# A hybrid delta-rule and S5 step: a new order of loads and of small work ahead of the first projection

## The reference, cut to what matters

```python
def ada_mod(c, w_mod, b_mod):
    m = (jax.nn.silu(c) @ w_mod + b_mod)[:, None, :]
    shift, scale, gate = jnp.split(m, 3, axis=-1)
...
    hn = rmsnorm(x, norm_mix[i]) * (1.0 + scale) + shift
    out, cv, sd = gdn_mixer(hn, ...)      # proj = hn @ w_in, then a short causal convolution
...
    dt = jnp.exp(log_dt)[:, None]         # S5 tables: no input x in them
    mag = jnp.exp(lr * dt); ang = li * dt
    ab_re, ab_im = mag * jnp.cos(ang), mag * jnp.sin(ang)
```

## Time and profile before

| | |
|---|---|
| median of 3 runs | 1769.54 us (1766.22 to 1769.86) |
| the profiled execution's own time | 1765.61 us |
| its span, first to last instruction | 1763.9 us |
| PE busy | 1484.9 us, 84% of the span |
| DVE busy | 709.5 us, 40% |
| ACT busy | 404.5 us, 23% |
| POOL busy | 116.6 us, 7% |
| mean granted clock of PE | 0.888 of full |
| PE's share of the chain that ended last | 49% |

### The profile page before, as it was taken

One profiled execution on the slowest core, in us unless ns is written; L12 is line 12 of the kernel. 1 busy time (PEld: TensorE's weight loads), 2 busy tenths in 40 slices (PEclk: granted clock), 3 DMA queues, 4 the chain that ended last, 5 costly groups with the idle time before them and its releaser, 6 DMA issues.

```text
span 1763.9 us, 26539 instructions
## 1 busy us (share of the span) xinstructions
PE 1484.9 (84%) x11278; PEld 1160.8 (66%) x11278; DVE 709.5 (40%) x1207; ACT 404.5 (23%) x559; POOL 116.6 (7%) x162
## 2 busy tenths in 40 slices
PE   3799999968876888965999958998999955999955
PEld 2577777746675826743878846776777734778744
DVE  1657895055553054144111147779701140111106
ACT  2344551013222010031011122462200131111102
POOL 0011122000000030002000020000000002000010
PEclk9899999978887557976999968999999967999986
DMA  6555519000002340127999772003012208999833
GB/s 249 213 227 218 201 48 374 39 1 2 3 3 79 125 143 24 52 116 289 347 363 351 269 262 103 1 1 144 3 48 72 79 3 316 347 357 352 302 142 116
DMA packets 66354, 281.42 MB, mean 160 GB/s; under 512 B 7248, under 2 KB 23888, under 8 KB 42576
## 3 DMA queue, kind: packets, MB, share of 16 engines
q1 hardware_dynamic: 60720, 260.08, 39.9%
q0 software_dynamic: 5536, 19.93, 3.2%
HBM read 228.24 MB, written 51.74 MB: 159 GB/s over the span
## 4 chain that ended last, share of the span: by engine, by line
PE 49%; DVE 9%; ACT 3%; DMA 3%; issue 3%; POOL 1%; SPq 0%; POOLq 0%; DVEq 0%; ACTq 0%
PE acc L664 14%; PE acc L989 14%; PE acc L997 7%; PE acc L1119 2%; PE acc L906 2%; PE acc L684 1%; PE acc L1085 1%; ACT hT L1253 1%; POOL xs L2358 1%; DMA yT<-xs 1%; PE acc L675 1%; PE acc L1196 1%; DVE zT L2092 1%; DMA xs<-big,row_of 1%; DMA big<-ys,row_of 1%
## 5 line engine op out<-in xcount | busy, mean ns | idle before, releaser
L664 PE MATMUL acc<-hT,ring 128*128 128x288 f32 x1792 | 442.1, 408 | 10.0 <-ACT hT L1253 7.8
L664 PEld LDWEIGHTS acc<-hT,ring 128*128 128x128 f32 x1792 | 340.7, 191 | 113.3 <-issue 9.8
L989 PEld LDWEIGHTS acc<-zT,ring 128*128 128x128 f32 x2176 | 253.7, 196 | 20.2 <-issue 14.3
L989 PE MATMUL acc<-zT,ring 128*128 128x128 f32 x2176 | 254.6, 279 | 4.6 <-ACT zT L1283 2.3
L997 PE MATMUL acc<-ring,zT 128*128 128x512 f32 x272 | 124.9, 602 | 8.6 <-DVE zT L2092 2.9
L2092 DVE TENSOR_TENSOR zT<-zT,acc 128x256 f32<-128x256 f32 x32 | 13.5, 421 | 235.1 <-ACT zT L1288 235.1
L997 PEld LDWEIGHTS acc<-ring,zT 128*128 128x128 f32 x272 | 48.9, 189 | 64.4 <-issue 62.1
L2097 DVE COPY yT<-acc 128x1024 f32<-128x1024 f32 x32 | 39.2, 1225 | 124.8 <-PE acc L997 124.8
L1288 ACT ACTIVATE zT<-acc 128x256 f32<-128x256 f32 x32 | 12.3, 383 | 316.5 <-PE acc L989 316.5
L980 PE MATMUL acc<-cst,yT 128*128 128x128 f32 x272 | 37.1, 282 | 38.9 <-DMA yT<-xs 38.9
L664 PE MATMUL acc<-yT,ring 128*128 128x288 f32 x256 | 64.1, 414 | 1.8 <-DVE yT L1972 1.8
(11 more groups left out here) (440 smaller groups left out, 1972.7 us busy)
## 6 DMA issues: line engine op xcount, KB each, us to landing
ring<-in_w SPq DMA_DIRECT2D x102, 1024.0 KB, 8.1
ring<-in_w_mod_mix SPq DMA_DIRECT2D x24, 1024.0 KB, 8.2
ring<-in_w_mod_ffn SPq DMA_DIRECT2D x24, 1024.0 KB, 6.9
yT<-xs SPq DMA_DIRECT2D x34, 512.0 KB, 8.8
ring<-in_w_in SPq DMA_DIRECT2D x16, 1024.0 KB, 9.0
ys<-yT SPq DMA_DIRECT2D x32, 512.0 KB, 8.2
xs<-S SPq DMA_DIRECT2D x3, 4096.0 KB, 26.1
ring<-in_glu SPq DMA_DIRECT2D x8, 1024.0 KB, 9.6
```

Source lines behind the costliest of these rows:

```text
L664: mm = pe.matmul(ps[:, b, 0:HT], w[:, k, :], rhs[:, k, HT * b:HT * b + HT], start=(k == 0), stop=(k == KD - 1))
L989: mm = pe.matmul(acc[:, H_ACC, x, P * f:P * (f + 1)], wv[:, f, k, :], xt[:, k, :], start=(k == 0), stop=(k == KD - 1), skip_group_check=True)
```

## The change

SP issues c alone first, then units 0 and 1, then x, then units 2 and 3, then the masks, biases and norm weights (on a semaphore of their own, `masks_in`), then units 4 to 7, and only then the other eleven small tables. PE runs adaLN block 0 ahead of the sums of squares and waits for the masks behind them. ACT squares x in eight pieces, each released by itself; its exponentials of `lam` and `hp` go behind `baq`, and its exponential and sines of the S5 angles into turn 8 of the loop. DVE adds the biases of adaLN blocks 0 and 1 before it scales x, writes `hT` of the prompt tokens for the last three of the eight pieces (ACT for the first five), and computes the S5 angles in turn 4 and the S5 tables in turn 19 of the loop.

```diff
@@ -46,6 +46,7 @@
...
+H_BY_SCALAR = 5
...
+        c_in, masks_in = sem("c_in"), sem("masks_in")
...
             def consts(dst, src):
                 sp.dma_start(dst, src).then_inc(consts_in, up(consts_in, by=16))
 
-            sp.dma_start(xT[:, :, :], d["xT"]).then_inc(x_in, 16)
-            consts(cT[:, :, :], d["cT"])
-            for dst, src in ((cst[:, :, :], "masks"), (bmod[:, :, :], "bmod"), (nrm[:, :, :], "nrm"),
-                             (w_ba[:, :, :], "w_ba"), (onrm[:, :], "onrm"), (s5d[:, :], "s5d"),
-                             (wr[:, :, :, :], "wr")):
...
-            book["consts"] = now(consts_in)
+            def small_consts():
+                for dst, src in ((w_ba[:, :, :], "w_ba"), (onrm[:, :], "onrm"), (s5d[:, :], "s5d"),
...
+                book["consts"] = now(consts_in)
...
-            for n in range(unit_no["w_in", 0, 0]):
+            sp.dma_start(cT[:, :, :], d["cT"]).then_inc(c_in, 16)
+            for n in range(2):
                 load(n)
+            sp.dma_start(xT[:, :, :], d["xT"]).then_inc(x_in, 16)
+            for n in range(2, 4):
+                load(n)
+            for dst, src in ((cst[:, :, :], "masks"), (bmod[:, :, :], "bmod"), (nrm[:, :, :], "nrm")):
+                sp.dma_start(dst, d[src]).then_inc(masks_in, 16)
+            for n in range(4, unit_no["w_in", 0, 0]):
+                load(n)
+            small_consts()
             sp.dma_start(cs_in, d["conv"]).then_inc(conv_in, up(conv_in, by=16))
...
                     for k in range(KD):
-                        pe.wait_ge(squares_ready, at(f"nsq{i}_{k if i else 0}"))
+                        pe.wait_ge(squares_ready, at(f"nsq{i}_{k}"))
...
-            pe.wait_ge(consts_in, book.get("consts", 16))
             pe.wait_ge(ones_ready, at("ones"))
-            norm_sums(0)
             pe.wait_ge(silu_c_ready, at("silu_c"))
             for nb in range(4):
                 adaln(0, nb)
-                if nb:
+                if nb == 0:
+                    norm_sums(0)
+                    pe.wait_ge(masks_in, 48)
+                else:
                     adaln_turn(0, nb - 1)
             adaln_turn(0, 3)
             await_input(0)
+            pe.wait_ge(consts_in, book.get("consts", 16))
             narrow("baq", w_ba[:, :, :].rearrange("p k c -> p (k c)"), 16)
...
-            act.wait_ge(consts_in, book.get("consts", 16))
...
-            act.wait_ge(x_in, 16)
-            act.activation(yT[:, :, :], xT[:, :, :], ACT.Square).then_inc(squares_ready, up(squares_ready, "nsq0_0"))
-            act.wait_ge(squares_ready, now(squares_ready))
-            act.wait_ge(acc_full, filled("ssq0"))
-            act.activation(halves(rb[:, :]), tok("ssq0"), ACT.Sqrt, bias=small[:, 0:1], scale=1.0 / D).then_inc(
-                act_drained, up(act_drained, "read:ssq0"))
-            act.wait_ge(act_drained, now(act_drained))
-
...
+            act.wait_ge(c_in, 16)
...
+            act.activation(c32[:, :, 0:9], cT[:, :, :], ACT.Silu).then_inc(silu_c_ready, up(silu_c_ready, "silu_c"))
+            act.wait_ge(silu_c_ready, now(silu_c_ready))
+
+            modulation(0, 0)
+            act.wait_ge(x_in, 16)
+            for k in range(KD):
+                act.activation(yT[:, k, :], xT[:, k, :], ACT.Square).then_inc(
+                    squares_ready, up(squares_ready, f"nsq0_{k}"))
+            act.wait_ge(squares_ready, now(squares_ready))
+            act.wait_ge(acc_full, filled("ssq0"))
+            act.activation(halves(rb[:, :]), tok("ssq0"), ACT.Sqrt, bias=small[:, 0:1], scale=1.0 / D).then_inc(
+                act_drained, up(act_drained, "read:ssq0"))
+            act.wait_ge(act_drained, now(act_drained))
+
+            for nb in range(1, 4):
                 modulation(0, nb)
             act.wait_ge(x_scaled, at("npre0"))
             act.wait_ge(mod_ready, at("mod0"))
-            for k in range(KD):
+            for k in range(H_BY_SCALAR):
                 ins = act.activation(hT[:, k, 0:SEQ], yT[:, k, 0:SEQ], ACT.Identity,
                                      bias=modT[:, 0, k, 0:1], scale=modA[:, 0, k, 0:1])
-                if k < KD - 1:
+                if k < H_BY_SCALAR - 1:
                     ins.then_inc(act_order, up(act_order))
...
+            act.wait_ge(consts_in, book.get("consts", 16))
+            step(act.activation(lam[:, 2, :], lam[:, 2, :], ACT.Exp))
+            act.activation(hp[:, 0, :], hp[:, 0, :], ACT.Exp).then_inc(dt_ready, up(dt_ready, "dt"))
+            act.wait_ge(dt_ready, now(dt_ready))
             act.wait_ge(gate_args_ready, at("ba"))
...
             for m in range(32 + 3):
+                if m == 8:
+                    act.wait_ge(s5_angle_ready, at("ang"))
+                    step(act.activation(s5t[:, 0, :], s5t[:, 0, :], ACT.Exp))
+                    step(act.activation(s5t[:, 3, :], s5t[:, 1, :], ACT.Sin))
+                    act.activation(s5t[:, 4, :], s5t[:, 2, :], ACT.Sin, bias=small[:, 2:3], scale=-1.0).then_inc(
+                        trig_ready, up(trig_ready, "trig"))
+                    act.wait_ge(trig_ready, now(trig_ready))
                 if m < QKV:
...
-            dve.wait_ge(consts_in, book.get("consts", 16))
-            dve.wait_ge(dt_ready, at("dt"))
-            lr, li, dt = lam[:, 0, :], lam[:, 1, :], lam[:, 2, :]
-            step(tt(s5t[:, 0, :], lr, dt, ALU.mult))
-            step(tt(s5t[:, 1, :], li, dt, ALU.mult))
...
-            dve.wait_ge(x_in, 16)
-            dve.wait_ge(act_drained, at("read:ssq0"))
-            step(dve.reciprocal(rb[:, :], rb[:, :]))
-            tt(yT[:, :, :], xT[:, :, :], bc(rb[:, :], 1, KD), ALU.mult).then_inc(x_scaled, up(x_scaled, "npre0"))
-            dve.wait_ge(x_scaled, now(x_scaled))
-
...
-            for nb in range(4):
+            dve.wait_ge(x_in, 16)
+            dve.wait_ge(act_drained, at("read:ssq0"))
+            step(dve.reciprocal(rb[:, :], rb[:, :]))
+            dve.wait_ge(masks_in, 48)
+            for nb in range(2):
+                modulation(0, nb)
+            tt(yT[:, :, :], xT[:, :, :], bc(rb[:, :], 1, KD), ALU.mult).then_inc(x_scaled, up(x_scaled, "npre0"))
+            dve.wait_ge(x_scaled, now(x_scaled))
+
+            for nb in range(2, 4):
                 modulation(0, nb)
             step(tt(seqs(hT[:, :, SEQ:T]), seqs(yT[:, :, SEQ:T]), bc(modA[:, 0, :, 1:9], 3, LS), ALU.mult))
-            tt(seqs(hT[:, :, SEQ:T]), seqs(hT[:, :, SEQ:T]), bc(modT[:, 0, 0:KD, 1:9], 3, LS), ALU.add).then_inc(
-                sample_input_ready, up(sample_input_ready, "hs0"))
+            start(tt(seqs(hT[:, :, SEQ:T]), seqs(hT[:, :, SEQ:T]), bc(modT[:, 0, 0:KD, 1:9], 3, LS), ALU.add))
+            for k in range(H_BY_SCALAR, KD):
+                ins = ts(hT[:, k, 0:SEQ], yT[:, k, 0:SEQ], modA[:, 0, k, 0:1], modT[:, 0, k, 0:1], ALU.mult, ALU.add)
+                if k < KD - 1:
+                    start(ins)
+            ins.then_inc(sample_input_ready, up(sample_input_ready, "hs0"))
+            dve.wait_ge(dve_order, now(dve_order))
             dve.wait_ge(sample_input_ready, now(sample_input_ready))
-            dve.wait_ge(trig_ready, at("trig"))
-            step(dve.memset(pw[:, 0, 0, :], 1.0))
-            step(dve.memset(pw[:, 1, 0, :], 0.0))
...
+                if m == 4:
+                    lr, li, dt = lam[:, 0, :], lam[:, 1, :], lam[:, 2, :]
+                    step(tt(s5t[:, 0, :], lr, dt, ALU.mult))
...
+                if m == 19:
+                    dve.wait_ge(trig_ready, at("trig"))
+                    step(dve.memset(pw[:, 0, 0, :], 1.0))
+                    step(dve.memset(pw[:, 1, 0, :], 0.0))
+                    ar, ai = pw[:, 0, 1, :], pw[:, 1, 1, :]
+                    step(tt(ar, s5t[:, 0, :], s5t[:, 4, :], ALU.mult))
+                    step(tt(ai, s5t[:, 0, :], s5t[:, 3, :], ALU.mult))
+                    t0, t1, t2 = s5t[:, 5, :], s5t[:, 6, :], s5t[:, 7, :]
+                    for r in range(1, 8):
+                        step(tt(t0, pw[:, 0, r, :], ar, ALU.mult))
+                        step(tt(t1, pw[:, 1, r, :], ai, ALU.mult))
+                        step(tt(pw[:, 0, r + 1, :], t0, t1, ALU.subtract))
+                        step(tt(t0, pw[:, 0, r, :], ai, ALU.mult))
+                        step(tt(t1, pw[:, 1, r, :], ar, ALU.mult))
+                        step(tt(pw[:, 1, r + 1, :], t0, t1, ALU.add))
...
+                    step(tt(fz[:, 1, :], t0, t2, ALU.mult))
+                    step(dve.tensor_copy(lr, s5t[:, 4, :]))
+                    step(dve.tensor_copy(li, s5t[:, 3, :]))
+                    dve.wait_ge(silu_c_ready, at("silu_c"))
+                    dve.tensor_copy(c32_kept, c32).then_inc(silu_c_kept, 1)
+                    dve.wait_ge(silu_c_kept, 1)
+
                 if 2 <= m < N_LATE + 2:
```

97 lines of the change are left out of this document (36 added, 61 removed).

## The result

The changed kernel takes 1750.04 us, the median of 4 runs (1749.12 to 1752.65); the kernel before, run beside it, 1768.69 (4 runs, 1766.22 to 1769.86). The ratio is 0.9899, 95% interval 0.9882 to 0.9916: 18.65 us less, by the interval 14.9 to 20.9. The profiled execution took 1752.65, with a span of 1751.0. In one of the later groups one execution of the kernel before took 2522.07 us at a mean granted clock of 0.577, and one of the kernel with only the tables moved 1920.22 at 0.781; the ratios are without them.

What follows compares the result with a forecast made beforehand. One chain of waits up to the loop was taken to bound the kernel: narrow projection at 42.95 instead of 59.25 us, gain 16.3, span 1763.9 to 1747.6; with overhead and median offset it took 1752 us, range 1745 to 1759.

Steps and rivals of the forecast that it cites:

- x's landing: Load of x behind c and two units: lands at 15.4 us, bounds 14.9 to 18.4.
- The squares in pieces: ACT's squares of x: 0.68 us a piece, PE's sums from 16.3 to 26.8; pieces give 3.4 us.
- Behind the sums: Root, reciprocal, two bias additions and scaling of x on DVE: from 26.8 to 38.2 us.
- `hT`: Writing the loop's input: ACT's five pieces end at 42.9, DVE's part at 42.2; narrow projection starts at 42.95 us.
- adaLN's slack: Last adaLN block on PE: turned at 37.1 us, needed at 38.2, 1.1 us of slack.
- Small tables: Eleven loads issued behind unit 7: issued by about 21 us, landed by about 34, hidden with 9 us of cover.
- ACT in turn 8: Exponential and sines in the loop: at most 2.2 us plus a 1.3 us table load, against 5.5 idle; cost 0.
- The tables in turn 19: S5 tables on DVE in the loop: 14.7 us, ACT's read of block 21 5 us late; cost 0.
- The gain of a full clock: More-gain rival: narrow projection at full clock on PE, 1.8 us more, 1750 us; chance 0.05.
- Less gain: Rival at the start: x lands at up to 18.4 or adaLN ends later; gain 11 to 13 us; chance 0.10.
- no gain: Rival: the loop gives the lead back because something else ends last; 1766 to 1771 us; chance 0.04.
- slower: Rival: PE's clock stays at half in the loop, 7.8 us more per projection; with five, 1775 us; chance 0.05.

Runs made afterwards that it cites:

- Turn 11: Changed kernel with the S5 tables on DVE in turn 11 of the loop instead of turn 19: 1766.23 us, ratio 0.9989.
- second profile of the changed kernel: The changed kernel run again with nothing altered, beside later runs: 1750.43 us, ratio 0.9898.
- x first with block 0 behind the sums: Changed kernel with x issued right behind c, ahead of all units, and adaLN block 0 behind the sums of squares: 1747.59 us, ratio 0.9887.
- near twin with four pieces: Kernel with x ahead of all units and block 0 behind the sums, with four `hT` pieces on ACT instead of five: 1750.37 us, ratio 0.99.

## Why the prediction was right

The mechanism held in each step; 18.0 us came out at the narrow projection where 16.3 were forecast, and 18.65 in the medians. Of the 1.7 us more at the narrow projection 1.0 is x's landing, 0.6 shorter sums and 0.1 the first piece. None of the three was foreseen, and 0.8 was lost again to the clock, so that the loop's 17.15 lies nearer to the forecast than its terms do; that much is luck.

- *x's landing* was the term most off: 14.4 us, forecast 15.4, outside its bounds of 14.9 to 18.4. By the measured rates (0.45 MB in the first 4 us, then 0.427 MB per us) x's bytes are through at 13.5, so the lag behind its own bytes was 0.9 us, not the 1.5 that x had before nor the 2.0 of unit 0. The 13.4 of a strict order was as near as my 15.4.
- *The squares in pieces*: first sums at 15.19 (16.3), 0.73 us behind ACT's start (0.83: a piece takes 0.59, not 0.68). The sums took 9.86 us, not 10.47, and this size moves by itself: 9.47 to 10.62 over these runs, with the number of opening matmuls that take 687 ns instead of 406 (below). Worth of the pieces 2.7 in the loop, forecast 3.4; the difference is within what the sums and the clock's return move by themselves.
- *Behind the sums*: the root's 2.25 us, the reciprocal's 3.75, the additions' 0.43 (forecast 0.45) and the scaling's 4.96 came to 0.02 us. 1.07 us from scaling to `hT`, forecast 1.1.
- *`hT`*: 3.63 on ACT as forecast, DVE's pieces 0.48 each (0.50), DVE done at 40.3 and ACT at 41.2: ACT the later, by 0.9 (0.7). Between a piece's bounds of 0.35 and 0.72 the price did not matter, as the text said.
- *adaLN's slack*: turned at 34.5 on PE, 2.0 us ahead of the scaling's end, forecast 1.1. No wait for unit 7. With block 0 behind the sums that slack was gone: there the last turn ended 0.1 us behind the scaling.
- *Small tables*: hidden, but with less cover than I gave. I priced SP's issues at 0.64 us, from fifteen transfers where there are sixteen (0.60); they took up to 2.24 (below), and SP was through with them at 30.09, not 21, so that they and not its slot (free by 26.9) set the issue of the loop's first unit. That unit landed about 40.1, needed at 45.27; the last table landed near 36.5, and PE waits for all of them at 41.27: about 5 us of cover, forecast 9.
- *ACT in turn 8* 3.4 us of work ahead of a read that still waits 2.09: cost 0. *The tables in turn 19*: block 21 about 6 us late (5), no idle time on PE: cost 0. Turn 11 showed what the same 15 us cost without cover.
- *Rivals*. The gain of a full clock did not come: the narrow projection ran at 0.50 and even lost 0.36 us. The price I had put on that was right in kind and low in size: 1.92 us from the narrow projection (4.07 to 2.15) and 0.46 from the first projection, against my 1.8. Less gain, no gain and slower did not come; the clock was back at 0.94 from 46 us.

In the loop 17.15 us are left, and in the profiled pair 12.9 of span. Of the 4.3 us between, 1.5 go in the stretch shown above and 2.8 behind 561.3 us, where the changed kernel's first profile is 1189.7 us long and the one before 1186.9; in the second profile of the changed kernel it is 1186.5. So the 2.8 move from execution to execution. The 1.5 are in both profiles of the changed kernel (219.10 us each, clock 0.81 as before) and stay unexplained. The medians, with their interval of 14.9 to 20.9 us, can't say whether they count.

The best version was x first with block 0 behind the sums, 1747.59 us, 2.5 to 2.8 below the changed kernel's medians; its own intervals and those of the changed kernel overlap, and its near twin with four pieces came to 1750.37. The trace gives it a lead of 2.9 us in the loop, but the near twin lost it to a later landing of unit 7, and I don't call it proven.

## What to carry to other kernels

At a start bound by one stream of loads, ask of each strand what it waits for last, and put its first bytes in that order; then look at what stands ahead of each long instruction: an addition of 0.2 us held the scaling of x up by 1.3 wherever the block that it needs was turned later. Where two strands end together, as with block 0 behind the sums, removing one wait shows nothing. Work moved into another engine's idle time costs nothing only if nothing that the busy engine needs is queued behind it: read that slack in the very turn where the work will stand. And a gain of 2 us at the front can vanish in a span of 1750 us, where the clock alone moves later stages by 3 to 4.
